# RWKV recurrence: the idle products beside its levels are left out

## The reference, cut to what matters

```python
def step(S, inp):
    r_t, w_t, k_t, v_t, a_t, b_t = inp
    sa = jnp.einsum("bhij,bhj->bhi", S, a_t)
    S = S * w_t[:, :, None, :] + sa[..., None] * b_t[:, :, None, :] + v_t[..., None] * k_t[:, :, None, :]
    y = jnp.einsum("bhij,bhj->bhi", S, r_t)
    return S, y
```

## Time and profile before

| | |
|---|---|
| profiled execution | 2074.06 us |
| span of the trace | 2072.3 us |
| mean granted TensorE clock | 0.989 |
| TensorE busy | 1995.8 us (96%) |
| VectorE, ScalarE, GpSimd busy | 1079.6, 924.3, 1280.3 us |
| the recurrence (first score to the end of the gate) | about 338 to 552 us |

### The profile page before, as it was taken

How to read it: one execution, slowest core, us unless ns; L and a number is a source line. 1 busy time by engine, 2 the same in 40 slices (tenths; PEclk the granted TensorE clock), 3 DMA queues, 4 the chain that set the end, 5 groups by cost and what they waited for, 6 DMA issues and landing times.

```text
span 2072.3 us, 44016 instructions
## 1 busy us (share of the span) xinstructions
PE 1995.8 (96%) x17510; PEld 1880.3 (91%) x17510; DVE 1079.6 (52%) x1648; ACT 924.3 (45%) x1618; POOL 1280.3 (62%) x528
## 2 busy tenths in 40 slices
PE   8999998999999999999998999999999989999997
PEld 8999787778799999999985999999998877899997
DVE  5781677566678726770366677112182244325431
ACT  4434552111343344333446543444446556555553
POOL 6888362000268887888640688968657654677885
PEclk9999999999999999999999999999999999999999
DMA  7455331000144554455320455544455332344552
GB/s 285 162 180 185 123 120 65 3 2 3 62 161 164 180 185 147 178 182 182 125 101 1 143 183 184 202 170 156 143 185 182 131 134 103 130 175 155 188 184 82
DMA packets 40937, 291.46 MB, mean 141 GB/s; under 512 B 4448, under 2 KB 5728, under 8 KB 5856
## 3 DMA queue, kind: packets, MB, share of 16 engines
q1 hardware_dynamic: 40512, 288.26, 38.8%
q10 hardware_dynamic: 288, 1.18, 0.2%
HBM read 288.38 MB, written 1.05 MB: 140 GB/s over the span
## 4 chain that ended last, share of the span: by engine, by line
PE 31%; issue 28%; POOLq 19%; POOL 19%; ACT 1%; DVE 1%; DVEq 0%; DMA 0%; ACTq 0%
POOLq L2010 19%; POOL w_low L2006 19%; PE ps L623 9%; PE ps L631 9%; PE ps L627 9%; PE ps L1378 2%; PE ps L1366 1%; PE ps L1356 1%; POOLq L2005 0%; PE ps L753 0%; ACT units L1912 0%; ACT units L1445 0%; POOLq L2022 0%; PE ps L734 0%; DMA con<-consts 0%
## 5 line engine op out<-in xcount | busy, mean ns | idle before, releaser
L2006 POOL TENSOR_TENSOR w_low<-wring,w_high 128x1024 fp32r<-128x1024 f32 x524 | 1280.1, 2458 | 771.8 <-ACT w_high L1445 740.8
L623 PE MATMUL ps<-in_high,w_high 128*128 128x256 f32 (+1 forms) x2856 | 824.8, 289 | 16.3 <-POOL w_low L2006 6.4
L631 PE MATMUL ps<-in_high,w_low 128*128 128x256 f32 (+1 forms) x2856 | 815.0, 285 | 0.0
L627 PE MATMUL ps<-in_low,w_high 128*128 128x256 f32 (+1 forms) x2856 | 813.0, 285 | 0.0
L1445 ACT ACTIVATE w_high<-wring 128x1024 fp32r<-128x1024 f32 x524 | 542.3, 1055 | 253.0 <-PE ps L623 247.6
L623 PEld LDWEIGHTS ps<-in_high,w_high 128*128 128x128 f32 x2856 | 539.7, 189 | 32.2 <-issue 18.9
L631 PEld LDWEIGHTS ps<-in_high,w_low 128*128 128x128 f32 x2856 | 540.0, 189 | 0.0
L627 PEld LDWEIGHTS ps<-in_low,w_high 128*128 128x128 f32 x2856 | 538.9, 189 | 0.4
L623 PE MATMUL ps<-hid_high,w_high 128*128 128x272 f32 (+1 forms) x880 | 250.5, 285 | 0.0
L631 PE MATMUL ps<-hid_high,w_low 128*128 128x272 f32 (+1 forms) x880 | 250.5, 285 | 0.0
L627 PE MATMUL ps<-hid_low,w_high 128*128 128x272 f32 (+1 forms) x880 | 250.0, 284 | 0.0
(11 more groups left out here) (344 smaller groups left out, 2578.8 us busy)
## 6 DMA issues: line engine op xcount, KB each, us to landing
wring<-stream SPq DMA_DIRECT2D x270, 1024.0 KB, 4.8
con<-consts SPq DMA_DIRECT2D x1, 2199.0 KB, 16.3
X<-x_in SPq DMA_DIRECT2D x1, 1088.0 KB, 7.9
units<-decay ACTq DMA_DIRECT2D x1, 1024.0 KB, 4.8
out<-AL SPq DMA_DIRECT2D x1, 1024.0 KB, 4.7
AL<-stream SPq DMA_DIRECT2D x2, 256.0 KB, 20.8
par<-params SPq DMA_DIRECT2D x1, 187.0 KB, 5.7
con<-consts ACTq DMA_DIRECT2D x1, 130.0 KB, 5.0
```

The costliest lines, as they stand in the source:

```text
L623: mm = pe.matmul(o, wh, high(k), start=(k == 0), stop=False)
L627: mm = pe.matmul(o, wh, low(k), start=False, stop=False)
L631: mm = pe.matmul(o, wl, high(k), start=False, stop=(k == kt - 1))
L2006: pool.tensor_tensor(w_low[:, (half + h) % SPLIT_RING, :], wring[:, slot, h * HALF * P:(h + 1) * HALF * P], w_high[:, (half + h) % SPLIT_R ...
```

## The change

Three calls of `fill` are taken out; nothing else changes.

```diff
                 for n in range(LEVELS):
                     chunks = [c for c in RK_ORDER if n < RK_LEVELS[c]]
                     for c in chunks:
-                        if g == n == 0:
-                            fill(4, 4)
                         if n == LEVELS - 1:
                             pe.wait_ge(S["rk_masked"], masked(g + 1, 2, 1) if g < 3 else len(MASKS))
-                            fill(7, 4)
                         rk_under(g, c, n)
                         yield
...
                         if i:
                             pe.wait_ge(S["rk_x0_added"], (g + 1) * RK_COUNT[0])
-                            fill(4, 4)
                         rk_score(after, 2, i)
```

## The result

The changed kernel took 2098.72 us (median of four, 2095.93 to 2103.1) against 2077.1 us for the kernel before (median of four, 2069.47 to 2083.58): a ratio of 1.0103, 95% interval 1.0075 to 1.0132. It is slower by about 1%. The profiled executions took 2096.13 and 2074.06 us, their spans 2094.3 and 2072.3: 22.0 us to be found.

The account below looks back on a forecast made before the run. TensorE, busy 96% at nearly full clock, was taken as the bound, also in most of the recurrence. -2.3 + 1.0 + 8.3 + 8.3 = +15.3 us on 2078.06 gave 2093.4 us, range 2074 to 2122.

Parts of the forecast that it names:

- The groups on the path: Second level-6 products of g = 1 to 3 start earlier without the removed groups: -2.3 us, clock effects apart.
- Where the clock falls: Level 6: the clock falls at g = 0 and once for g = 1 and 2 together, 8.3 us each.
- The price of a fall: After level 6, 10.4 us of work at half clock, each us costing 0.8 more: 8.3 us for a fall.
- The start: Start of g = 0: without three groups the clock stays low longer, slowing the merges from 356.47 to 360.3: +1.0 us.
- The gate at g = 3: After level 6 of g = 3 the clock falls a few us later anyway: nothing added, 5 us at most.
- The base: Whole kernel: the sum was set on 2078.06 us, the middle of the profiled time and the median.
- Rival 1: Level 6: clock holds or is back after short low stretches, not slower: 2075.8 or 2081.3 us; chance 0.27.
- Rival 2: Recurrence: once down, the clock stays down through most level stages, much slower: 2125 us; chance 0.10.
- Rival 3: Recurrence: removed groups were on the path more than shown, clearly faster, at most -17.1: 2061 us; chance 0.05.

Follow-up runs that it names:

- The last kernel: Kernel before, with both level-6 groups at g = 0, one at g = 1 to 3, none elsewhere, six idle products at the recurrence's end: 2074.13 us, ratio 0.9981.

## Why the prediction was right

The forecast was a fall of the clock at g = 0 and at one of g = 1 and 2, 2093.4 us, slower. The trace has the fall at g = 0, a long one at g = 2 and a short one at g = 1, and the measured time is 2098.7. By the steps of the sum (+15.3 us, against 22.0 between the two traces):

- *The groups on the path, -2.3.* Right in mechanism and near in size. The second level-6 products of g = 1 to 3 gain 0.45, 0.45 and 1.17 us in the changed kernel's trace, 2.1 together. The last kernel, in which the clock holds from level 6 of g = 0 on and these same three groups are out, keeps 2.0 of it at the merges.
- *Where the clock falls.* Right at g = 0: it fell there in all six profiled kernels that had fewer than two 128-row groups in that step and in none of the five that had both. For g = 1 and 2 the prediction counted one fall between none and two. Both came, a long one and a short one, and in the kernel without the level-6 groups the long one was at g = 1 in place of g = 2. That a single count of 8.3 came out near was in part luck.
- *The price of a fall, 8.3.* Measured 6.3 at g = 0 for 17.0 us low and 9.6 at g = 2 for 23.8: 0.37 and 0.40 us for each us at half clock, where the factor of 1.8 gives 0.44. The length behind the 8.3 is 18.7 us (10.4 of work at half clock), a little long for g = 0 and too short for g = 2. Together the two falls cost 15.9 against 16.6, since the errors went opposite ways.
- *The short fall at g = 1.* It cost 1.6 us and is in no term of the sum.
- *The start, +1.0.* Wrong. The changed kernel seems to bear it out (1.3 us late at the merge of g = 0), but 0.9 of that was there at the last masked score, before the first removed group, behind a short low stretch (the 0.94 from 340 to 350 is its end); and with only these groups out the output projection is 0.1 us late. VectorE covers the whole of the start.
- *The gate at g = 3, nothing.* Wrong by 2.7 us: the fall there now lasts 17.2 us in place of 10.3. It stood as an end (5) and not in the sum.
- *The base.* The sum stood on 2078.06; the median with more runs is 2077.1. The 2.6 us that the changed kernel loses behind the output projection are in no term either.

Rival 1 had named its own test, a clock of 1.00 at 389.6 us and behind, and the trace shows 0.50 there; the kernels without the level-6 groups and with the 16-row products show it again. Rival 2, the clock that stays down, did not happen. The clock came back at about 406 at g = 0, where the first 128-row solve starts at 404.47, and at about 515 at g = 2, 8 us behind the first one (507.19); at g = 1 it was back by 447, with only the 128-row variance products before. The products put behind the merges bear out that 128-row work brings it back; how soon it does so differs from place to place. Rival 3 had nothing for it.

The Trainium skill (TensorE: Matmul & The Clock Gate, why this matters for your kernels) asks that no long idle gap open between bursts of matmuls; that rule taken alone would have made this change a gain. The trace speaks against taking it alone: TensorE's longest gap ahead of the fall at g = 0 is 1.94 us, and with the 16-row products in place, where the longest wait ahead of the fall in that step is 0.75 us, the clock fell too. The prediction's own evidence for this, the fall at 346 behind gaps of 1.33 us at most, holds only from 340 us on: a gap of 1.86 us ends at 337.84.

## What to carry to other kernels

A product whose result nobody reads may be what keeps TensorE at full speed: before one is taken out, look for the sparse stretch that it fills, count what is left there in products and rows, and look for the granted clock in the rows where similar work stood alone. Where VectorE ends last anyway, a low clock costs nothing and the filler can go; where TensorE works without a pause behind the sparse stretch, one fall costs far more than the filler. Here a group on the path cost 0.4 to 1.2 us and the others nothing, while a long fall cost some 5 to 10 us. Products put behind the sparse stretch gave back less than a third of the loss (1.0073 against 1.0103).

## What the runs showed of the hardware that was not expected

The length of a record does not decide: 16-row products of the same length, 1.15 us for eight records, did not hold the clock where 128-row ones did. Whether it is the rows in use or the nonzero values in them is not shown.

A short sparse stretch can be followed by a long time at half clock: behind the 2 to 4 us of level 6 the low stretches lasted 3.4 to 23.8 us, and in the long ones TensorE was busy nearly all of the time with products of 16 and 64 rows (10.00 of 10 us from 500 to 510 in the changed kernel, at 0.50).

The kernel before spreads over 2068 to 2087 us from run to run, and the recurrence need not be the reason. The kernel without the start's groups begins the output projection 0.1 us later than the kernel before and ends its span 10.2 us later (2082.5 against 2072.3). First of the kernel before, then of that one, two stretches far behind the recurrence:

```profile
1050.00:1200.00 150.00, 137.16 (x942) 0.95 0.23 80
1700.00:1760.00 60.00, 54.97 (x407) 0.97 0.30 106
```

```profile
1050.00:1200.00 150.00, 137.99 (x912) 0.92 0.22 77
1700.00:1760.00 60.00, 52.94 (x350) 0.89 0.30 106
```

The same work found a lower clock there: about 15 us low against 24 in the first stretch, 3.6 against 13 in the second, while nothing in these stages was changed. In the profile of the last kernel the clock was 0.90 in both. The 72 executions of the kernel before that were taken beside the experiments agree: the four fastest (2068.2 to 2068.6 us) had a mean granted clock of 0.992, the four slowest (2083.7 to 2087.1 us) 0.980 or 0.981. The 2.6 us that the changed kernel lost behind the output projection may be of this kind, since the change does not touch these stages; this was not followed further.
